# Projecting all latent-attention heads in a stage of their own, instead of inside the attention loop

## The reference

```python
def mla(q_lat, kv_lat, k_rope, q_norm_g, w_qb, kv_norm_g, w_kvb):
    b, l = q_lat.shape[:2]
    q = (rms_norm(q_lat, q_norm_g) @ w_qb).reshape(b, l, MLA_HEADS, MLA_NOPE + MLA_ROPE)
    kv = (rms_norm(kv_lat, kv_norm_g) @ w_kvb).reshape(b, l, MLA_HEADS, MLA_NOPE + MLA_V)
    q_nope, q_pe = q[..., :MLA_NOPE], q[..., MLA_NOPE:]
    k_nope, v = kv[..., :MLA_NOPE], kv[..., MLA_NOPE:]
    q_pe = apply_rope(q_pe, cos[:, None, :], sin[:, None, :])
    ...
        s = (jnp.einsum('bqhd,bkhd->bhqk', qn_b, k_nope)
             + jnp.einsum('bqhd,bkd->bhqk', qp_b, k_pe)).astype(jnp.float32)
        p = jax.nn.softmax(s, axis=-1).astype(v.dtype)
        return jnp.einsum('bhqk,bkhd->bqhd', p, v)
```

## Time and profile before

| | us |
|---|---|
| median of 3 runs (4335.8 to 4348.6) | 4338.3 |
| the profiled execution | 4340.0 |
| its span, first to last instruction | 4338.2 |
| PE busy in the span | 4046.4 |
| DVE busy | 2574.0 |
| ACT busy | 1979.0 |
| `mla_stage`, from its first DMA (1962.6) to the last head's end (about 4098) | 2136 |
| of it before the first score (2058.3) | 96 |

### The profile page before, as it was taken

One profiled execution on the slowest core, in us unless ns is written; L12 is line 12 of the kernel. 1 busy time (PEld: TensorE's weight loads), 2 busy tenths in 40 slices (PEclk: granted clock), 3 DMA queues, 4 the chain that ended last, 5 costly groups with the idle time before them and its releaser, 6 DMA issues. The chain is left out here.

```text
span 4338.2 us, 55444 instructions
## 1 busy us (share of the span) xinstructions
PE 4046.4 (93%) x18296; PEld 2996.9 (69%) x18296; DVE 2574.0 (59%) x4425; ACT 1979.0 (46%) x3184; POOL 971.0 (22%) x520
## 2 busy tenths in 40 slices
...
GB/s 271 134 83 64 73 64 61 42 142 143 117 117 119 137 89 0 74 54 26 6 14 9 11 14 14 9 14 9 11 14 14 9 14 9 11 14 12 32 164 124
DMA packets 219766, 253.54 MB, mean 58 GB/s; under 512 B 103215, under 2 KB 179055, under 8 KB 213511
## 3 DMA queue, kind: packets, MB, share of 16 engines
...
## 5 line engine op out<-in xcount | busy, mean ns | idle before, releaser
L1559 ACT ACTIVATE ml_p_f<-ml_scores 128x1024 f32<-128x1024 f32 (+1 forms) x528 | 535.3, 1014 | 740.4 <-PE ml_scores L1414 703.0
L1385 POOL TENSOR_TENSOR ml_p_lo<-ml_p_f,ml_p_hi 128x1024 fp32r<-128x1024 f32 x256 | 620.9, 2425 | 834.9 <-ACT ml_p_hi L1560 820.2
L1624 DVE TENSOR_REDUCE ml_peaks<-ml_aux 128x1 f32<-128x512 f32 x1024 | 677.1, 678 | 149.2 <-PE ml_aux L1414 144.4
L1560 ACT ACTIVATE ml_p_hi<-ml_scores 128x1024 fp32r<-128x1024 f32 (+1 forms) x528 | 531.3, 1006 | 0.0
L1661 DVE TENSOR_TENSOR ml_p_lo<-ml_p_f,ml_p_hi 128x1024 fp32r<-128x1024 f32 (+1 forms) x272 | 378.0, 1390 | 174.1 <-ACT ml_p_hi L1560 165.4
L1414 PE MATMUL ml_aux<-ml_k_hi,ml_q_hi 96*128 96x512 f32 (+1 forms) x1056 | 443.8, 429 | 21.9 <-DVE ml_peaks L1624 21.6
L1414 PE MATMUL ml_scores<-ml_q_hi,ml_k_hi 97*128 97x512 f32 (+1 forms) x1056 | 447.2, 424 | 16.5 <-issue 13.6
L546 DVE TENSOR_TENSOR pr_x_lo<-hT,pr_x_hi 128x512 fp32r<-128x512 f32 (+1 forms) x280 | 179.1, 640 | 439.3 <-ACT pr_x_hi L536 439.2
L1414 PE MATMUL ml_out_ps<-ml_p_hi,ml_v_hi 128*128 128x512 f32 (+1 forms) x1056 | 425.5, 403 | 13.5 <-POOL ml_p_lo L1385 10.3
L1414 PE MATMUL ml_out_ps<-ml_p_lo,ml_v_hi 128*128 128x512 f32 (+1 forms) x1056 | 418.0, 396 | 0.0
L1414 PE MATMUL ml_scores<-ml_q_lo,ml_k_hi 97*128 97x512 f32 (+1 forms) x1056 | 413.6, 392 | 0.0
...
## 6 DMA issues: line engine op xcount, KB each, us to landing
mod_w<-in_ada_w SPq DMA_DIRECT2D x12, 2048.0 KB
...
pr_w_raw<-in_ev_w SPq DMA_DIRECT2D x6, 2048.0 KB, 8.2
...
x_in<-in_x_sample SPq DMA_DIRECT2D x4, 2048.0 KB, 12.1
...
```

The costliest lines, as they stand in the source:

```text
L1385: nc.gpsimd.tensor_tensor(p_lo[:, n % 3, 0:w], p_f[:, (s * NU + n) % 2, 0:w], p_hi[:, n % 3, 0:w].bitcast(FP32), ALU.subtract).then_inc(lo ...
L1559: nc.scalar.activation(p_f[:, (s * NU + n) % 2, 0:w], src[:, 0:w], ACT.Exp).then_inc(exp_done, 1)
L1560: nc.scalar.activation(p_hi[:, n % 3, 0:w], src[:, 0:w], ACT.Exp).then_inc(exp_done, 1)
L1624: nc.vector.reduce_max(peaks[:, col:col + 1], src[:], AX.X).then_inc(prep_dve, 1)
```

## The change

All projections leave the loop. A new stage `heads_stage` stands between the gate projection and `mla_stage`. It loads the weights of all heads (5 DMAs of 512 KB), splits them and the latents into fp32r parts, and works through five chunks of tokens (four of 512, one of 256). Per chunk of 512: 8 "plain" tiles (query dimensions without rotation, two heads to a tile; 6 matmuls each), 4 "turned" tiles (the 32 rotated dimensions of four heads; 6 matmuls), 8 "key" tiles (3 matmuls) and 8 "value" tiles (3 matmuls). ACT copies plain and key tiles out of PSUM, DVE value tiles; a turned tile takes three products on DVE and a sum on POOL. The results go into 16 places of 512 columns (a ring of 4 groups of 4 tiles) and by DMA to DRAM: one store for a plain, key or value tile (the value store in pieces of 256 bytes), eight of 16 rows for a turned one. A place can be filled again once all stores of its group have landed; PE has 8 PSUM tiles.

`mla_stage` loads the four parts of a head (2.1 MB) into `q_raw`, `k_raw`, `v_raw` while the head two before it runs, and its 15 tasks are now splits alone, with no matmul: ACT rounds from SBUF, DVE subtracts in SBUF. The rotations on DVE, POOL and ACT are gone. Three splits stand in each of steps 2 to 6, and the 65 peak tasks in steps 7 to 29. Weight loads per head and the rotation table are gone; the latents' space is given back before `mla_stage`.

```diff
+def heads_stage(nc, a, m):
...
+    QC_, GROUP, RING = 12 * P, 4, 4
+    PARTS = (2 * QC_ + 2 * D) // CH
+    TILES = []
+    for c, (c0, n) in enumerate(CHUNKS):
+        TILES += [("plain", c, f) for f in range(8)] + [("turned", c, f) for f in range(4)] + [("key", c, f) for f in range(8)]
+        TILES += [("value", c, f) for f in range(2 * (n // P))]
...
+    STORES = {"plain": 1, "turned": 8, "key": 1, "value": 1}
...
+        def slot_free(eng, e):
+
+            g = e // GROUP
+            if g < RING:
+                eng.wait_ge(w_lo_done, PARTS)
+            else:
+                eng.wait_ge(stored[g % RING], stores_until(g - RING))
...
+                elif kind == "turned":
+                    sp.wait_ge(pool_out, by_pool[e])
+                    for h in range(4):
+                        for half in range(2):
+                            sp.dma_start(m.q_turned[2 * f + h // 2, h % 2, half * 16:(half + 1) * 16, c0:c0 + n],
+                                         place(e)[half * HD + h * 16:half * HD + (h + 1) * 16, 0:n]).then_inc(done, 16)
+                else:
+                    sp.wait_ge(dve_out, by_dve[e])
+                    t, half = c0 // P + f // 2, f % 2
+                    dst = m.v_heads[4 * half:4 * half + 4, :, :, t].rearrange("j s p d -> p (j s) d")
+                    sp.dma_start(dst, place(e).rearrange("p (h d) -> p h d", d=HD)).then_inc(done, 16)
...
+                if e >= 8:
+                    if TILES[e - 8][0] in ("plain", "key"):
+                        pe.wait_ge(act_out, by_act[e - 8])
+                    else:
+                        pe.wait_ge(dve_out, by_dve[e - 8])
...
+                    for r in ((2,) if kind == "key" else (0, 1)):
+                        (l_h, l_l), (w_h, w_l) = lat(r), col(at + (r * QC_ if r < 2 else 0), P)
+                        terms += [(w_h, l_h[:, 0:n]), (w_h, l_l[:, 0:n]), (w_l, l_h[:, 0:n])]
+                for i, (lhsT, rhs) in enumerate(terms):
+                    last = nc.tensor.matmul(ps[e % 8][:, 0:n], lhsT, rhs, start=(i == 0), stop=(i == len(terms) - 1))
+                last.then_inc(tile_done, 1)
...
+                    nc.vector.tensor_tensor(along[:, s, 0:n], ps[e % 8][:, 0:n], wave[:, c % 2, 0, 0:n], ALU.mult)\
+                      .then_inc(dve_out, 1)
+                    for h in range(2):
+                        src, dst = slice(h * HD, (h + 1) * HD), slice((1 - h) * HD, (2 - h) * HD)
+                        nc.vector.tensor_tensor(across[dst, s, 0:n], ps[e % 8][src, 0:n], wave[src, c % 2, 1, 0:n], ALU.mult)\
+                          .then_inc(dve_out, 1)
...
+                    nc.vector.tensor_copy(place(e), ps[e % 8][:]).then_inc(dve_out, 1)
...
+                    nc.gpsimd.tensor_tensor(place(e)[:, 0:n], along[:, f % 2, 0:n], across[:, f % 2, 0:n], ALU.add)\
+                      .then_inc(pool_out, 1)
...
+    FIRST, LAST_STEP = 2 + (NS + 2) // 3, NU - 4
     POINT_TASKS = [[[] for _ in range(4)] for _ in range(NU + LAG)]
     for i in range(N_TASKS):
-        if i < PROJ:
-            at = 4 * (1 + i // 2) + 1 + 2 * (i % 2)
+        if i < NS:
+            at = 4 * (2 + i // 3) + 1 + i % 3
         elif i < N_TASKS - 1:
-            at = 4 * FIRST + (i - PROJ) * 4 * (LAST_STEP + 1 - FIRST) // (N_TASKS - 1 - PROJ)
+            at = 4 * FIRST + (i - NS) * 4 * (LAST_STEP + 1 - FIRST) // (N_TASKS - 1 - NS)
         else:
...
+            def load(j, s):
+                for dst, src in ((q_raw[0:HD], m.q_nope[j, s * HD:(s + 1) * HD]), (q_raw[HD:MLA_K], m.q_turned[j, s]),
+                                 (k_raw[:], m.k_nope[j, s * HD:(s + 1) * HD]), (v_raw[:], m.v_heads[j, s])):
+                    sp.dma_start(dst, src).then_inc(raw_in, 16)
+
+            def load_ahead(j, s):
+
+                sp.wait_ge(started, 1)
+                sp.wait_ge(prep_dve, (2 * j + s - 1) * N_TASKS + (NS + DVE0))
+                load(j, s)
...
-            def rotate_sum(H, c):
...
-            def rotate_lo(H, s, c):
...
+                if i < NS:
+                    return
+                dst = aux[(i - NS) % 2]
+                pe.wait_ge(prep_dve, H * N_TASKS + ((i - 1 if i >= NS + 2 else 0) + DVE0))
+                if i == NS:
+                    pe.wait_ge(prep_act, H * NS + 2 * NCH)
...
+                if i == 0:
+                    act.wait_ge(raw_in, H * 64 + 64)
+                    if not first:
+                        act.wait_ge(pv_done, (H - 1) * NU + PV0)
...
+                nc.scalar.activation(into, src, ACT.Copy).then_inc(prep_act, 1)
...
+            heads_stage(nc, a, m)
+            latents.close()
             mla_stage(nc, a, m)
...
```

More of the change, by code:

```diff
@@ L102, in shape_constants @@
         "rope_k": np.concatenate([cos, sin]),
[L103 removed]
+        "rope_q": wave,
     }
```

307 lines of the change are left out of this document (168 added, 139 removed).

## The result

The changed kernel takes 4378.4 us (median of 4 runs, 4374.3 to 4383.6), the kernel before 4339.4 on the same chip. The ratio is 1.0087, 95% interval 1.0066 to 1.0108: slower, by 39 us, where 4304 and a gain of 35 were forecast.

The account below looks back on a forecast made before the run. The prediction took PE to bound the attention loop. From 4340 us it took 189 for the loop and 21 for head 0's preparation and added 176 for the new stage: 4306, as a median 4304 us, range 4260 to 4350.

Parts of the forecast that it names:

- What bounds the kernel: Attention loop: PE sets the time; a step without tasks takes 2.8 us, the projection tasks cost 16.56 us a head.
- Wait in step 3 for ACT's copy: Loop: `weigh` of the first large unit waits for ACT's copy of the prompt's sums, 1.0 to 2.0, taken as 1.6 us.
- Wait in step 6 for the `p_lo` of unit 4: Loop: `weigh` of unit 4 waits for its `p_lo` from DVE, 0.8 to 2.0, taken as 1.6 us.
- Wait in step 7 for the first maximum: Loop: the third peak task waits for DVE's maximum of the first, 1.7 us.
- The old wait in steps 9 to 12: Loop, steps 9 and 11: today's 1.9 us wait of PE for DVE's pile shrinks by 1.1 us.
- Gain per head: Loop: each of 15 prepared heads gains 12.6 us, 189 us together, bounds 158 to 225.
- The rule weighed: Loop: DVE splits of two SBUF tiles contend with POOL; at 1.5 times their length, 8.4 us gained per head, 4367 us.
- Head 0's preparation: Before head 0's first peak: preparation falls from 40 to 19 us, gain 21, range 15 to 25.
- The new stage: `heads_stage`: 22 us lead-in, four chunks of 31 us, last chunk 30.5 us; 176 us in all, range 161 to 202.
- Rival 1: New stage: SP and the DMA queue set its pace; stage 233 us, time 4361 us; chance 0.08.
- rival 2: Loop: the contention rule holds for every split on DVE; time 4367 us; chance 0.04.
- The fourth case: Partly Rival 1 or rival 2: stage at 200 us, or 11.3 us gained per head; about 4326 to 4330 us; chance 0.18.

Follow-up runs that it names:

- experiment 8: The changed kernel with DVE's 15 splits placed by POOL's free time (behind the even `p_lo` in steps 3 and 5, otherwise ending even steps): 4304.0 us.
- Experiment 4: The changed kernel, but the loop's ten query and key splits on DVE read one SBUF and one PSUM tile and write zeros: 4371.7 us.
- experiment 3: The changed kernel with 24 places instead of 16 in the new stage's ring: 4380.5 us.
- experiment 5: The changed kernel, but the `p_lo` of units 3 and 5 are made by DVE instead of POOL: 4369.4 us.
- experiment 7: The changed kernel with DVE's splits two behind every even unit's `p_lo`, steps 3 to 17; ACT's roundings and peaks stay: 4416.9 us.
- Experiment 12: The kernel of experiment 8 with five extra ACT copies at the end of step 5 in each of 15 heads, to pause PE: 4394.6 us.

## Why the prediction was wrong, step by step

- **What bounds the kernel** (PE in the loop, one step of 2.8 us, the 16.56 us of projections): borne out. Where DVE's order avoids POOL (experiment 8) a head takes 115.1 us on average, against 129.7 before: 14.6 gained where 12.6 were forecast. The 115.4 of the prediction is no mark for that average. It starts from head 13's 128.0, and the even heads from 2 to 12, at whose end the loop's body turns, take 132.
- **Wait in step 3 for ACT's copy**, taken as 1.6: right in kind, a little more in size; PE stands 2.07 us for `ml_summed_p` in head 12, 1.97 on average of 15 heads.
- **Wait in step 6 for the `p_lo` of unit 4**, taken as 1.6: this step failed; it is 5.23. DVE's pile was counted at the durations of operations that meet nobody; two of its nine splits were held, 4.35 us. On the prediction's own clock, from the end of the scores of unit 2 (3691.1), the `p_lo` was to be done after 13.6 to 14.8 us and was done after 17.7, while PE was there after 12.5, about as forecast (11.2 and the 1.6 already waited).
- **Wait in step 7 for the first maximum**, 1.7: not there, because PE came later itself. In its place stood the clock: up to 2.8 us that no term of the sum had. So units 1 to 9 take 4.7 us more than forecast (32.7 against 28).
- **The old wait in steps 9 to 12**, 1.1 of 1.9 gone: more went. Units 9 and 12 lie 10.4 us apart in head 12, where they lay 12.4, so all of it is gone.
- **Gain per head** 12.6: measured 9.75, 146 us instead of 189, below the lower bound of 158, and a head takes over the 118 named as the mark. The heads are not alike: head 0, without reciprocals, gains 13.1, heads 6 to 13 gain 9.2 each, and head 13, from which the forecast was read, only 7.1 (127.7 to 120.6).
- **The rule weighed** named the right mechanism with the wrong law. I priced it as 1.5 times on each split, discounted that to 1.5 us per head by the share of time in which POOL is busy, and put none of it into the 12.6. But a hold lasts until POOL's operation ends, whatever the split's own length, and in this packed row on DVE a split stood where POOL began in all 15 heads. The rows that I used already said so, as the 53 `p_lo` above show. The Trainium skill, in SBUF — State Buffer, section SBUF: two separate sides, states it: of a GpSimd operation and a DVE operation with two SBUF inputs, whichever starts first has the shared pair of ports for its whole instruction, and the other is blocked. The trace agrees (2.89 against 0.68, 2.55 against 0.41). The Trainium skill, in SBUF — State Buffer, section Who interferes with whom, states that a DVE instruction with at most one SBUF input does not contend, leaving DVE's two-port modes aside. Experiment 4 agrees: 0.67 us under POOL's work.
- **Head 0's preparation**, gain 21: right, 23.4.
- **The new stage**, 176: this step failed too; 210.2. The lead-in was 18 us to the first matmul (22 forecast), the last chunk 31.0 from its first store (30.5 forecast, from PE's start); the chunks, forecast at 31 each, put their first stores 43.5, 38.1, 38.2 and 37.6 us apart. The mis-sized term is SP's price of a store: plain 0.80 to 0.86, turned 0.49 to 0.51, key 0.69 to 0.76, value 1.09 to 1.14 us in the chunks of 512 behind the first, where 0.45, 0.45, 0.45 and 0.53 were taken. I had bounded these from rows of an idle queue and of a full one and took the idle one, though the same paragraph had the DMA engines at 22 of 31 us. The ring, to which I gave the space, plays no part (experiment 3).
- **The rivals.** Rival 1 (SP and the queue pace the stage) and rival 2 (the contention) both came, at 0.6 and 0.7 of their price. Each by itself would have put the kernel at 4338 or 4347, about where it was. The fourth case held "partly 1 or 2", one of them and not both (its own numbers make 4328 and 4324, not 4326 to 4330); the case with both, at 4378, had no place in the list, nor in the range, though nothing made the two exclude each other.
- **Hidden loads:** right; nothing waits for `q_raw` inside the loop.

What stays open: how the loop's missing 43 us divide between holds, backlog and clock in the changed kernel. Experiments 4, 5, 7 and 8 and head 0 show that holds and backlog feed each other: head 0 has holds and no reciprocals and loses nothing. Experiment 12 has 1.3 us beyond ACT's delay at one pause of PE, but does not part the clock from what ACT and DVE hide. A kernel with the same pile and no POOL work at all wasn't tried.
